# Hybrid attention and mLSTM layer on one core: the first projection block split by k, its neighbour in other PSUM banks

## The chip, the cores and the metric

The kernel runs on one core of one Trainium2 chip. The metric is the device time of one execution in microseconds (us), the median over several executions.

## The reference, cut to what matters

One layer over 256 tokens of width 1024, batch 1. After a norm, a single projection `w_in` gives all inputs of two mixers; its products and four elementwise steps are what the change touches:

```python
h = rms_norm(x, mix_norm_g[layer])
proj = h @ w_in[layer]                     # 1024 -> 5640 features
(q_a, k_a, v_a, q_m, k_m, v_m, o_m, i_m, f_m, g_a, g_m) = jnp.split(proj, split_points, axis=-1)
y_a = from_heads(moba_attention(...))      # 8 heads of 64
qk_m = jax.nn.silu(causal_depthwise_conv(jnp.concatenate([q_m, k_m], axis=-1), conv_qk[layer]))
log_i = (i_m.astype(f32) + b_igate[layer].astype(f32)).transpose(0, 2, 1)
log_f = jax.nn.log_sigmoid(f_m.astype(f32) + b_fgate[layer].astype(f32)).transpose(0, 2, 1)
h_m = mlstm_chunkwise(...)                 # 4 heads of 128
merged = sigmoid(g_a) * (y_a @ w_out_attn) + sigmoid(g_m) * (y_m @ w_out_mlstm)
x = x + merged @ w_o[layer]
h = rms_norm(x, ffn_norm_g[layer])
x = x + (silu(h @ w_ffn_gate[layer]) * (h @ w_ffn_up[layer])) @ w_ffn_down[layer]
return rms_norm(x, final_norm_g)
```

The convolution runs over time, 4 taps wide, on the 512 features of `q_m` and the 512 of `k_m`.

## The kernel before, in words

All products are made in three passes of a rounded type: each operand is split into a high part (`w_hi`, `hT_hi`) and the rest (`w_lo`, `hT_lo`), and hi x hi, hi x lo and lo x hi are summed in PSUM. The 1024 x N weights come in **chunks** of 128 x 2048 numbers (1 MB), 63 in the whole kernel. A chunk c goes through four steps: SyncE loads it into one of three raw buffers (`load`; it waits until the chunk three before has its low part, `lo_ready`), ScalarE copies it to `w_hi` (`split_hi`, `hi_ready`), VectorE subtracts to get `w_lo` (`split_lo`, `lo_ready`), TensorE uses it and counts `chunk_used`. Six slots hold hi and lo parts.

Every engine runs its own list of instructions in the order in which it is written, and waits on counters. ScalarE and VectorE have a loop over chunks c in which the split of chunk c + 4 stands beside the other work of step c.

The order of the blocks is `q_m` (chunks 0 and 1), `k_m` (2, 3), `q_a` (4, 5), `k_a` (6, 7), then token-major blocks. For the first eight chunks the weights are the stationary operand, so a result tile is 128 features x 256 tokens. Chunk 0 holds 256 features and all eight k-tiles. TensorE turns x (8 k-tiles x 2 token tiles, each 128 x 128) into the banks named `xT`; ScalarE scales and rounds them into `hT_hi` (`xT_hi`), VectorE makes `hT_lo` (`xT_lo`). Chunk 0 is loaded in three pieces (two of 256 KB, one of 512 KB); the low parts of the two small ones are made by GpSimd (L385), that of the third by VectorE (L868). While TensorE is in chunk 0, it also transposes `vec_rows`, the convolution's weights (L1259), and VectorE copies them to `vcol` (L872) before `split_lo(1)`. The eight gate columns (`wif`) are split by ScalarE and VectorE (L549, L551, L877) and multiplied in `gates`, after chunk 1.

The convolution of chunk c (0 to 3) is `tap3(c)` on ScalarE and `conv(c)` on VectorE, six instructions (L739, counted by `conv_step`), which read the chunk's PSUM bank. Chunk c + 4 is written to the same bank, and so TensorE waits there: `pe.wait_ge(conv_step, 6 * (c - 3))` for c from 4 to 7. The gate rows (L891 to L895), a logarithm on ScalarE (L562, L564) and the scans over time (L900 to L908) all stand in VectorE's step c == 2. `gate_columns` on TensorE comes after chunk 5 and uses them.

Of the kernel before, what the change touches and what calls it, by code (L numbers as in the profile page):

```python
# [62 lines left out]
def build(nc, x, mix_norm_g, w_in, conv_qk, b_igate, b_fgate, mlstm_norm_g, w_out_attn,  # L63
# [11 lines left out]
    with ExitStack() as ctx:  # L75
# [211 lines left out]
        def _(sp):  # L287
            def load(c, src):
# [138 lines left out]
        def _(act):  # L427
# [23 lines left out]
            def tap3(c):  # L451

                b, h = divmod(c, 2)
                act.wait_ge(chunk_used, c + 1)
                if c == 0:
# [1015 lines left out]
```

## Time and profile before

| | us |
|---|---|
| runs of the kernel before (3) | 394.48 median, 394.45 to 396.41 |
| profiled execution, its own time | 395.16 |
| span of that execution, first to last instruction | 393.1 |
| TensorE busy with products | 381.3 (97%) |
| VectorE busy | 241.7 (62%) |
| ScalarE busy | 199.6 (51%) |
| GpSimd busy | 35.2 (9%) |
| TensorE's first product of chunk 0 starts | 11.03 |

The page gives for each engine how long it was busy. The trace below it lists instructions with their start (us from the start of the span), how long they took, and in brackets how long the engine had been idle and what ended that. The tables of waits and the chain of work that ended last say which wait was the last to end.

### The profile page before, as it was taken

What the parts mean: (1) busy time and instruction counts of PE and PEld (TensorE: products, weight loads), DVE (VectorE), ACT (ScalarE), POOL (GpSimd) and SP (SyncE); (2) the same over time, 40 slices, a digit from 0 to 9 for tenths busy, and PEclk for the clock granted to TensorE, in tenths of its full rate; (3) what the DMA queues carried; (4) which work ended last, traced back from release to release, by engine and by line L of the source; (5) the groups of instructions that cost most, each with busy time, mean ns of one, the idle gap of its engine ahead of it and who ended that gap; (6) DMA issues with size and microseconds to landing.
All of it is one profiled execution on the core that took longest, in us unless ns stands there. A gap on an engine that the chain in (4) does not pass through costs nothing.

```text
span 393.1 us, 5336 instructions
## 1 busy us (share of the span) xinstructions
PE 381.3 (97%) x2101; PEld 326.8 (83%) x2101; DVE 241.7 (62%) x312; ACT 199.6 (51%) x246; POOL 35.2 (9%) x46
## 2 busy tenths in 40 slices
PE   6999999999999999999999999999999999999993
PEld 5999998777888888887878888888888888888882
DVE  2869777748529677569458573735648366472224
ACT  5862997554676546063347472552716437163014
POOL 3896001000000010000110000000000000000002
PEclk9999999999999999999999999999999999999997
DMA  7889076943534589627234848448184572930002
GB/s 248 244 278 306 10 229 226 334 168 113 179 137 152 176 316 321 214 82 243 105 107 159 269 147 281 150 172 267 68 305 128 192 238 85 316 106 1 0 0 108
DMA packets 48697, 70.55 MB, mean 179 GB/s; under 512 B 2300, under 2 KB 33064, under 8 KB 48680
## 3 DMA queue, kind: packets, MB, share of 16 engines
q1 hardware_dynamic: 48520, 70.05, 53.6%
q8 instruction: 12, 0.20, 0.2%
q10 hardware_dynamic: 160, 0.27, 0.2%
q14 instruction: 5, 0.04, 0.0%
HBM read 69.26 MB, written 1.05 MB: 179 GB/s over the span
## 4 chain that ended last, share of the span: by engine, by line
PE 85%; DVE 7%; DMA 3%; ACT 2%; issue 1%; POOL 0%; SPq 0%; POOLq 0%; ACTq 0%
PE pa L1102 19%; PE pp L1111 13%; PE pp L1112 13%; PE pp L1113 13%; PE pa L1104 10%; DVE w_lo L718 3%; PE pa L1111 2%; PE pa L1112 2%; PE pa L1113 2%; DMA w_raw<-in_w_in 2%; DVE region_a L739 2%; DMA x_sb<-in_x 1%; PE pp L1082 1%; ACT w_hi L433 1%; PE pp L1084 1%; PE pp L1083 1%
## 5 line engine op out<-in xcount | busy, mean ns | idle before, releaser
L718 DVE TENSOR_TENSOR w_lo<-w_raw,w_hi 128x2048 fp32r<-128x2048 f32 x38 | 86.8, 2295 | 36.2 <-ACT w_hi L433 36.2
L433 ACT ACTIVATE w_hi<-w_raw 128x2048 fp32r<-128x2048 f32 x38 | 72.8, 1918 | 25.4 <-PE pp L1113 14.8
L1102 PE MATMUL pa<-hT,w_hi 128*128 128x512 f32 x320 | 79.9, 392 | 0.0
L1102 PEld LDWEIGHTS pa<-hT,w_hi 128*128 128x128 f32 x320 | 58.2, 189 | 10.8
L1038 DVE TENSOR_TENSOR w_lo<-w_raw,w_hi 128x2048 fp32r<-128x2048 f32 x24 | 53.6, 2288 | 8.9 <-ACT w_hi L684 8.9
L1111 PE MATMUL pp<-w_hi,hT 128*128 128x512 f32 x128 | 51.1, 400 | 0.0
L1113 PE MATMUL pp<-w_lo,hT 128*128 128x512 f32 x128 | 49.9, 390 | 0.0
L1112 PE MATMUL pp<-w_hi,hT 128*128 128x512 f32 x128 | 49.9, 390 | 0.0
L1104 PEld LDWEIGHTS pa<-hT,w_lo 128*128 128x128 f32 x320 | 43.7, 190 | 3.1
L1104 PE MATMUL pa<-hT,w_lo 128*128 128x256 f32 x320 | 44.6, 282 | 0.0
L684 ACT ACTIVATE w_hi<-w_raw 128x2048 fp32r<-128x2048 f32 x24 | 44.1, 1902 | 0.0
L1111 PE MATMUL pp<-w_hi,yT_hi 128*128 128x512 f32 x104 | 40.7, 391 | 0.0
L1112 PE MATMUL pp<-w_hi,yT_lo 128*128 128x512 f32 x104 | 40.6, 390 | 0.0
L1113 PE MATMUL pp<-w_lo,yT_hi 128*128 128x512 f32 x104 | 40.5, 389 | 0.0
L1021 DVE TENSOR_TENSOR region_a<-pa,region_a 128x512 f32<-128x512 f32 x10 | 6.9, 692 | 44.6 <-ACT region_a L666 44.6
L666 ACT ACTIVATE region_a<-pa 128x512 f32<-128x512 f32 x10 | 6.0, 599 | 47.3 <-PE pa L1104 47.3
L1111 PEld LDWEIGHTS pp<-w_hi,hT 128*128 128x128 f32 x128 | 24.1, 188 | 5.9 <-issue 1.3
L1113 PEld LDWEIGHTS pp<-w_lo,hT 128*128 128x128 f32 x128 | 24.0, 188 | 5.2
L1082 PE MATMUL pp<-hT,w_hi 128*128 128x256 f32 x96 | 27.3, 284 | 0.7 <-DVE region_a L739 0.7
L1112 PEld LDWEIGHTS pp<-w_hi,hT 128*128 128x128 f32 x128 | 24.1, 188 | 4.6
L1084 PE MATMUL pp<-hT,w_lo 128*128 128x256 f32 x96 | 27.2, 283 | 0.0
L1083 PE MATMUL pp<-hT,w_hi 128*128 128x256 f32 x96 | 27.2, 283 | 0.0
(218 smaller groups left out, 524.9 us busy)
## 6 DMA issues: line engine op xcount, KB each, us to landing
w_raw<-in_w_in SPq DMA_DIRECT2D x21, 1024.0 KB, 5.1
w_raw<-in_w_ffn_gate SPq DMA_DIRECT2D x11, 1024.0 KB, 5.4
w_raw<-in_w_ffn_up SPq DMA_DIRECT2D x11, 1024.0 KB, 6.2
w_raw<-in_w_ffn_down SPq DMA_DIRECT2D x11, 1024.0 KB, 6.5
w_raw<-in_w_o SPq DMA_DIRECT2D x4, 1024.0 KB, 5.8
w_raw<-in_w_out_attn SPq DMA_DIRECT2D x2, 1024.0 KB, 5.0
w_raw<-in_w_out_mlstm SPq DMA_DIRECT2D x2, 1024.0 KB, 5.1
x_sb<-in_x SPq DMA_DIRECT2D x4, 256.0 KB, 3.8
```

Source lines behind the costliest of these rows:

```text
L433: nc.scalar.activation(w_hi[:, slot_of(c), :], w_raw[:, c % RAW, :], ACT.Copy).then_inc(hi_ready, 1)
L684: nc.scalar.activation(w_hi[:, slot_of(c + r), :], w_raw[:, (c + r) % RAW, :], ACT.Copy).then_inc(hi_ready, 1)
L718: nc.vector.tensor_tensor(w_lo[:, slot_of(c), :], w_raw[:, c % RAW, :], w_hi[:, slot_of(c), :].bitcast(F32), ALU.subtract).then_inc(lo_rea ...
L1038: nc.vector.tensor_tensor(w_lo[:, slot_of(c + r), :], w_raw[:, (c + r) % RAW, :], w_hi[:, slot_of(c + r), :].bitcast(F32), ALU.subtract).t ...
L1082: mm(o, hi[:, w], hT_hi[:, k, :], start=(k == 0), stop=False)
L1083: mm(o, hi[:, w], hT_lo[:, k, :], start=False, stop=False)
L1084: ins = mm(o, lo[:, w], hT_hi[:, k, :], start=False, stop=(k == KT - 1))
L1102: mm(banks[:, f, :], w_hi[:, s, w[k]], hT[:, k], start=(k == 0), stop=False)
L1104: ins = mm(banks[:, f, 0:S], w_lo[:, s, w[k]], hT_hi[:, k, :], start=False, stop=(k == KT - 1))
L1111: mm(o, aT_hi[:, k, tok], w_hi[:, s, w], start=start, stop=False)
L1112: mm(o, aT_lo[:, k, tok], w_hi[:, s, w], start=False, stop=False)
L1113: return mm(o, aT_hi[:, k, tok], w_lo[:, s, w], start=False, stop=stop)
```

## The change

- **Block 0 split by k.** Chunk 0 now holds k-tiles 0 to 3 for all 512 features of `q_m`, chunk 1 holds k-tiles 4 to 7. All four result tiles grow together, one in the first half of each of the four banks `pp`, over both chunks (`all_tiles`). For each k-tile there are eight products with `w_hi` before the four with `w_lo`.
- **Order on TensorE.** It turns x for k-tiles 0 to 3 of both token tiles and 4 to 7 of the first, then works on chunk 0; the last four transposes (`turn_x(1, 1)`) stand between chunk 0's hi and lo products. The transposes of `vec_rows` move from chunk 0 to chunk 1, behind its hi products.
- **Block 1 (`k_m`)** goes to the banks `pa` 0 and 1, and the waits of chunks 4 to 7 on `conv_step` become 6, 6, 12, 12 (they were 6, 12, 18, 24).
- **Gate rows in two parts.** The first part (the sums up to `row_l`) stands in VectorE's step c == 1, the scans stay in step c == 2. The gates use `pa` 2, `rcol` is turned in `pp` 3.
- **Loads.** x comes in two loads of 512 KB (was four of 256 KB), chunk 0 in two of 512 KB; the vector loads are issued by ScalarE instead of SyncE. Norms change places: ScalarE does the second half of the features, VectorE the first.
- **GpSimd** makes no low parts; VectorE makes both halves of chunk 0's.

```diff
-        xT = [pa[:, 0, 0:S], pp[:, 1, 0:S], pp[:, 2, 0:S], pp[:, 3, 0:S],
-              pa[:, 2, 0:S], pa[:, 3, 0:S], pa[:, 2, S:2 * S], pa[:, 3, S:2 * S]]
-
-        def conv_in(c, f):
-            if c == 0 and f == 1:
-                return pa[:, 1, 0:S]
-            return pp[:, c, f * S:(f + 1) * S]
+        xT = [pa[:, k % 4, k // 4 * S:(k // 4 + 1) * S] for k in range(KT)]
+
+        def conv_in(ft):
+            if ft < 4:
+                return pp[:, ft, 0:S]
+            return pa[:, ft // 2 - 2, ft % 2 * S:(ft % 2 + 1) * S]
...
-                if b < FEATURE_MAJOR:
+                if 0 < b < FEATURE_MAJOR:
                     return w_in_k[:, :, BLOCKS[b] + 256 * h:BLOCKS[b] + 256 * (h + 1)]
                 return w_in_k[:, 4 * h:4 * h + 4, BLOCKS[b]:BLOCKS[b] + 512]
...
-                    sp.wait_ge(piece_lo, 2)
+                    sp.wait_ge(first_half_lo, 1)
                 if c == 0:
-                    for n, loaded in enumerate((*piece_loaded, chunk_loaded[0])):
-                        part = slice(PIECES[n], PIECES[n + 1])
-                        sp.dma_start(as_source(w_raw[:, 0, part], src), src[:, PIECES[n] // 256:PIECES[n + 1] // 256]
-                                     ).then_inc(loaded, 16)
+                    sp.dma_start(as_source(w_raw[:, 0, 0:CH // 2], src), src[:, 0:2]).then_inc(first_half_loaded, 16)
+                    sp.dma_start(as_source(w_raw[:, 0, CH // 2:CH], src), src[:, 2:4]).then_inc(chunk_loaded[0], 16)
...
-            for t in range(T):
-                for h in range(2):
-                    sp.dma_start(x_t[:, t, HALVES[h]], x_d[:, t, HALVES[h]]).then_inc(x_loaded[t][h], 16)
+            sp.dma_start(x_t[:, 0], x_d[:, 0]).then_inc(x_loaded[0], 16)
+            sp.dma_start(x_t[:, 1], x_d[:, 1]).then_inc(x_loaded[1], 16)
             for c in range(C_FFN + 2):
                 load(c, chunk_source(c))
-                if c == 0:
-                    sp.dma_start(vec_rows[0:4, :], mlstm_norm_g.rearrange("a (h p) -> (a h) p", p=P)).then_inc(vec_loaded, 16)
-                    sp.dma_start(vec_rows[4:36, :], conv_qk.rearrange("a j (f p) -> (a j f) p", p=P)).then_inc(vec_loaded, 16)
+                if c == 1:
...
-            for n in range(2):
-                part = slice(PIECES[n], PIECES[n + 1])
-                pool.wait_ge(piece_hi[n], 1)
-                nc.gpsimd.tensor_tensor(w_lo[:, 0, part], w_raw[:, 0, part], w_hi[:, 0, part].bitcast(F32),
-                                        ALU.subtract).then_inc(piece_lo, 1)
...
             nc.scalar.activation(sinv[:, 0:8], minus_half[:, :], ACT.Square)
+            act.dma_start(vec_rows[0:4, :], mlstm_norm_g.rearrange("a (h p) -> (a h) p", p=P)).then_inc(vec_loaded, 16)
+            act.dma_start(vec_rows[4:36, :], conv_qk.rearrange("a j (f p) -> (a j f) p", p=P)).then_inc(vec_loaded, 16)
...
-            norm_half0(0)
-            act.wait_ge(piece_loaded[0], 16)
-            nc.scalar.activation(w_hi[:, 0, 0:512], w_raw[:, 0, 0:512], ACT.Copy).then_inc(piece_hi[0], 1)
-            norm_half0(1)
+            norm_half1(0)
+            act.wait_ge(first_half_loaded, 16)
+            nc.scalar.activation(w_hi[:, 0, 0:512], w_raw[:, 0, 0:512], ACT.Copy).then_inc(row_hi[0], 1)
             act.wait_ge(gcol_set, 1)
             for k in range(4):
                 xT_hi(k)
             act.wait_ge(chunk_loaded[0], 16)
             nc.scalar.activation(w_hi[:, 0, CH // 2:CH], w_raw[:, 0, CH // 2:CH], ACT.Copy).then_inc(hi_ready, 1)
+            norm_half1(1)
+            split_hi(1)
             for k in range(4, KT):
                 xT_hi(k)
-            for c in range(1, AHEAD):
+            for c in range(2, AHEAD):
...
-                if c == 2:
-
-                    act.wait_ge(gate_rows_set, 1)
-                    nc.scalar.activation(row_l, row_l, ACT.Exp).then_inc(exp1_done, 1)
...
+                if c == 3:
+                    tap3(3)
                 split_hi(c + AHEAD)
 
-                if c < 4:
-                    tap3(c)
-                elif c < 8:
+                if c == 1:
+                    tap3(0)
+                    tap3(1)
+
+                    act.wait_ge(gate_rows_set, 1)
+                    nc.scalar.activation(row_l, row_l, ACT.Exp).then_inc(exp1_done, 1)
...
+                elif c == 2:
+                    tap3(2)
...
+            def all_tiles(c, w_part, x_part, k):
+
+                for f in range(4):
+                    o = 512 * (k % 4) + f * P
+                    ins = mm(pp[:, f, 0:S], w_part[:, c, o:o + P], x_part[:, k, :],
+                             start=(k == 0 and w_part is w_hi and x_part is hT_hi),
+                             stop=(k == KT - 1 and w_part is w_lo))
+                return ins
...
+            turn_x(0, 0)
+            turn_x(0, 1)
+            turn_x(1, 0)
...
+                pe.wait_ge(conv_step, 12)
...
+                if c < 2:
+                    for k in range(4 * c, 4 * c + 4):
+                        if k < 2:
+                            pe.wait_ge(row_hi[k], 1)
+                        elif k in (2, 4):
+                            pe.wait_ge(hi_ready, c + 1)
+                        pe.wait_ge(hT_hi_set, k + 1)
+                        all_tiles(c, w_hi, hT_hi, k)
+                        pe.wait_ge(hT_lo_set, k + 1)
+                        all_tiles(c, w_hi, hT_lo, k)
+                    if c == 0:
+                        turn_x(1, 1)
+                    else:
+                        pe.wait_ge(vec_loaded, 32)
+                        nc.tensor.transpose(pa[:, 3, 0:36], vec_rows, ident[0:36, 0:36]).then_inc(vec_turned, 1)
+                    for k in range(4 * c, 4 * c + 4):
+                        if k == 0:
+                            pe.wait_ge(first_half_lo, 1)
+                        elif k in (2, 4):
+                            pe.wait_ge(lo_ready, c + 1)
+                        ins = all_tiles(c, w_lo, hT_hi, k)
                     ins.then_inc(chunk_used, 1)
                 elif b < FEATURE_MAJOR:
                     if b >= 2:
-                        pe.wait_ge(conv_step, 6 * (c - 3))
-                    feature_chunk(c, pp[:, 2 * (b % 2) + h, :]).then_inc(chunk_used, 1)
+                        pe.wait_ge(conv_step, 6 * (b - 1))
+                    if c == 7:
+                        pe.wait_ge(rcol_set, 1)
+                    feature_chunk(c, pa[:, h, :] if b == 1 else pp[:, 2 * (b % 2) + h, :]).then_inc(chunk_used, 1)
```

On VectorE, the start of the program. `w_lo` of 128x1024 is half of chunk 0, of 128x2048 a whole chunk (the first is chunk 1), `hT` rows are the k-tiles of x, `vcol` the convolution's weights, `w_ml` and `yT_hi` the gate columns. Before:

```order
L859 TENSOR_SCALAR region_b<-x_sb,rstd 128x512 [waits rstd_done] x2
L862 CAST w_hi<-w_raw 128x512 [waits piece_loaded1]
L844 SCALAR_TENSOR_TENSOR hT<-pa,gcol,hT 128x256 [waits hT_hi_set,gcol_set]
L844 SCALAR_TENSOR_TENSOR hT<-pp,gcol,hT 128x256 [waits hT_hi_set] x3
L844 SCALAR_TENSOR_TENSOR hT<-pa,gcol,hT 128x256 [waits hT_hi_set] x4
L868 TENSOR_TENSOR w_lo<-w_raw,w_hi 128x1024 [waits hi_ready]
L872 COPY vcol<-pp 128x36 [waits vec_turned]
L718 TENSOR_TENSOR w_lo<-w_raw,w_hi 128x2048 [waits hi_ready]
```

And in the changed kernel:

```order
L845 TENSOR_SCALAR region_b<-x_sb,rstd 128x512 [waits rstd_done] x2
L848 CAST w_hi<-w_raw 128x512 [waits first_half_loaded]
L830 SCALAR_TENSOR_TENSOR hT<-pa,gcol,hT 128x256 [waits hT_hi_set,gcol_set]
L830 SCALAR_TENSOR_TENSOR hT<-pa,gcol,hT 128x256 [waits hT_hi_set] x3
L854 TENSOR_TENSOR w_lo<-w_raw,w_hi 128x1024 [waits row_hi1,row_hi0]
L857 TENSOR_TENSOR w_lo<-w_raw,w_hi 128x1024 [waits hi_ready]
L830 SCALAR_TENSOR_TENSOR hT<-pa,gcol,hT 128x256 [waits hT_hi_set] x4
L863 COPY vcol<-pa 128x36 [waits vec_turned]
L705 TENSOR_TENSOR w_lo<-w_raw,w_hi 128x2048 [waits hi_ready]
```

The low parts of chunk 0 moved ahead of the last four k-tiles; the copy of `vcol` stands, as before, ahead of the low part of chunk 1.

On TensorE, around the transposes of `vec_rows` (`pT`). Before, they stand in chunk 0, ahead of its last eight lo products, and the 32 hi and 16 lo products of chunk 1 follow:

```order
L1259 MATMUL pp<-ident,pT 128x36 [waits vec_loaded]
L1088 MATMUL pp<-hT,w_lo 128x256 [waits lo_ready]
...
L1088 MATMUL pp<-hT,w_hi 128x256 [waits hi_ready,vcol_set]
L1088 MATMUL pp<-hT,w_hi 128x256 x15
L1088 MATMUL pp<-hT,w_lo 128x256 [waits lo_ready]
L1088 MATMUL pp<-hT,w_lo 128x256 x7
L1088 MATMUL pp<-hT,w_hi 128x256 x16
```

And in the changed kernel, from the last k-tile of chunk 1 on:

```order
L1088 MATMUL pp<-hT,w_hi 128x256 [waits hT_lo_set]
L1088 MATMUL pp<-hT,w_hi 128x256 x3
L1263 MATMUL pa<-ident,pT 128x36 [waits vec_loaded]
L1088 MATMUL pp<-hT,w_lo 128x256 [waits lo_ready]
L1088 MATMUL pp<-hT,w_lo 128x256 x15
L1147 MATMUL pa<-hT,yT_hi 100x256 [waits wif_lo_set,wif_hi_set]
```

The transposes moved behind all 32 hi products of chunk 1; only its 16 lo products are left between them and the gates.

## Rows read from the trace of the kernel before

**Rows 1.** Page: span, busy time, VectorE's row of low parts (busy us, mean ns)

```profile
span 393.1 us, 5336 instructions
PE 381.3 (97%) x2101; PEld 326.8 (83%) x2101; DVE 241.7 (62%) x312; ACT 199.6 (51%) x246; POOL 35.2 (9%) x46
...
L718 DVE TENSOR_TENSOR w_lo<-w_raw,w_hi 128x2048 fp32r<-128x2048 f32 x38 | 86.8, 2295 | 36.2 <-ACT w_hi L433 36.2
```

**Rows 2.** Table of waits, TensorE's products (us in total, times, longest)

```profile
PE pa L1136 <- ACT region_b L513: 1.6, 2, 0.8
PE pp L1082 <- DVE region_a L739: 0.7, 1, 0.7
PE pa L1111 <- DVE hT L725: 0.7, 1, 0.7
PE pa L1136 <- DVE region_b L859: 0.3, 1, 0.3
```

**Rows 3.** Timeline, third convolution and chunk 6 (start, us, engine, line; [idle before])

```profile
47.40 2.43 DVE L739 SCALAR_TENSOR_TENSOR region_a<-pp,vcol,region_a 128x255 f32<-128x255 f32 x6
48.99 0.26 PE L1161 MATMUL pa<-ident,v_ml 4*128 4x4 f32 x2
49.98 0.35 PE L1082 MATMUL pp<-hT,w_hi 128*128 128x256 f32 x1 [0.72 <-DVE region_a L739]
```

**Rows 4.** Timeline, TensorE and VectorE, 15 to 26 us

```profile
15.09 1.22 DVE L868 TENSOR_TENSOR w_lo<-w_raw,w_hi 128x1024 fp32r<-128x1024 f32 x1
16.15 0.25 PE L1259 MATMUL pp<-ident,pT 36*128 36x36 f32 x1
16.44 0.20 DVE L872 COPY vcol<-pp 128x36 f32<-128x36 f32 x1
16.55 2.28 DVE L718 TENSOR_TENSOR w_lo<-w_raw,w_hi 128x2048 fp32r<-128x2048 f32 x1
19.15 0.17 DVE L884 COPY w_ml<-w_ml 128x32 f32<-128x32 f32 x1
19.23 2.28 DVE L718 TENSOR_TENSOR w_lo<-w_raw,w_hi 128x2048 fp32r<-128x2048 f32 x1
21.43 0.75 DVE L877 TENSOR_TENSOR yT_hi<-w_ml,yT_hi 128x288 fp32r<-128x288 f32 x1
23.18 0.28 PE L1145 MATMUL pa<-hT,yT_hi 128*100 128x256 f32 x1
25.06 0.28 PE L1082 MATMUL pp<-hT,w_hi 128*128 128x256 f32 x1
```

**Rows 5.** Timeline, all engines, 7 to 12 us

```profile
7.26 0.69 DVE L854 CUSTOM_DVE_ANT_0 o_sb<-x_sb 128x512 f32<-128x512 f32 x1 [1.60 <-DMA x_sb<-in_x]
7.88 0.48 DVE L859 TENSOR_SCALAR region_b<-x_sb,rstd 128x512 f32<-128x512 f32 x1
8.42 0.66 PE L1136 MATMUL pa<-ident,region_b 128*128 128x128 f32 x4 [0.25 <-DVE region_b L859]
9.01 1.27 POOL L385 TENSOR_TENSOR w_lo<-w_raw,w_hi 128x512 fp32r<-128x512 f32 x1
9.08 1.48 DVE L859 TENSOR_SCALAR region_b<-x_sb,rstd 128x512 f32<-128x512 f32 x1 [0.72 <-POOL rstd L379]
9.86 0.33 PE L1136 MATMUL pa<-ident,region_b 128*128 128x128 f32 x1 [0.78 <-ACT region_b L513]
10.29 0.47 ACT L523 ACTIVATE hT<-pa,gcol 128x256 fp32r<-128x256 f32 x1 [0.48 <-PE pa L1136]
10.66 1.20 ACT L523 ACTIVATE hT<-pp,gcol 128x256 fp32r<-128x256 f32 x3
11.03 0.36 PE L1088 MATMUL pp<-hT,w_hi 128*128 128x256 f32 x1
11.73 1.07 ACT L542 ACTIVATE w_hi<-w_raw 128x1024 fp32r<-128x1024 f32 x1
```

**Rows 6.** Stretches of the load phase (first figure us, last two: DMA share, GB/s)

```profile
2.00:7.00 5.00, 4.73 (x24) 4.13 (x22) 0.87 (x3) 2.71 (x7) 0.74 (x2) 1.00 0.91 277
7.00:10.00 3.00, 1.43 (x9) 0.98 (x10) 2.02 (x4) 1.75 (x3) 1.81 (x3) 1.00 1.08 364
```

**Rows 7.** Timeline, small loads' issues, ScalarE ahead of x, GpSimd's long row

```profile
2.73 0.21 ACT L527 ACTIVATE sinv<-minus_half 128x8 f32<-128x8 f32 x1
4.16 0.45 SPq L308 DMA_DIRECT2D pT<-in_mlstm_norm_g  x1
4.65 0.66 SPq L309 DMA_DIRECT2D pT<-in_conv_qk  x1
15.24 15.90 POOL L404 TENSOR_SCALAR alibi<-w_ml 128x384 bf16<-128x384 f32 x8
```

**Rows 8.** Load of a chunk: issue in the timeline, time from issue to landing

```profile
27.46 0.37 SPq L300 DMA_DIRECT2D w_raw<-in_w_in  x1
DMA to landing us min/median/max: 5.3/5.3/5.3
```

**Rows 9.** Timeline, VectorE's gate rows with one row of ScalarE behind

```profile
36.91 0.46 DVE L891 TENSOR_SCALAR o_sb<-pa,b_if 4x256 f32<-4x256 f32 x1
38.79 0.41 DVE L895 SCALAR_TENSOR_TENSOR o_sb<-o_sb 4x256 f32<-4x256 f32 x1
39.23 0.42 ACT L562 ACTIVATE o_sb<-o_sb 4x256 f32<-4x256 f32 x1 [7.37 <-DVE o_sb L895]
```

More of the change, by code:

```diff
@@ L54 @@
 WARM = 23
-PIECES = (0, 512, 1024, CH)
 AHEAD = 4
@@ L194, in build @@
         squares_warm = sem("squares_warm")
-        piece_loaded = [sem(f"piece_loaded{n}") for n in range(2)]
-        piece_hi = [sem(f"piece_hi{n}") for n in range(2)]
-        piece_lo = sem("piece_lo")
+        first_half_loaded = sem("first_half_loaded")
+        row_hi = [sem(f"row_hi{k}") for k in range(2)]
+        first_half_lo = sem("first_half_lo")
         vec_turned = sem("vec_turned")
@@ L449, in turn_hi, with tap3 @@
                                          banks[b].rearrange("p (k n) -> p k n", k=4), ACT.Copy).then_inc(hT_hi_set, 1)
[L451 to L455, printed above, removed]
+            def tap3(n):
+                act.wait_ge(chunk_used, max(n + 1, 2))
+                if n == 0:
                     act.wait_ge(vcol_set, 1)
-                for f in range(2):
-                    ft = 4 * b + 2 * h + f
+                for ft in (2 * n, 2 * n + 1):
                     col = 4 + 3 * 8 + ft
-                    ins = nc.scalar.activation(qk_m[:, ft, :], conv_in(c, f),
-                                               ACT.Copy, scale=vcol[:, col:col + 1])
+                    ins = nc.scalar.activation(qk_m[:, ft, :], conv_in(ft), ACT.Copy, scale=vcol[:, col:col + 1])
                 ins.then_inc(tap3_done, 1)
@@ L858, in _ @@
                 dve.wait_ge(rstd_done, t + 1)
-                nc.vector.tensor_scalar(rb_t[:, t, HALVES[1]], x_t[:, t, HALVES[1]], rstd[:, t:t + 1], None,
-                                        ALU.mult).then_inc(half1_normed, 1)
-            dve.wait_ge(piece_loaded[1], 16)
-            nc.vector.tensor_copy(w_hi[:, 0, 512:1024], w_raw[:, 0, 512:1024]).then_inc(piece_hi[1], 1)
+                nc.vector.tensor_scalar(rb_t[:, t, HALVES[0]], x_t[:, t, HALVES[0]], rstd[:, t:t + 1], None,
+                                        ALU.mult).then_inc(half0_normed, 1)
+            dve.wait_ge(first_half_loaded, 16)
+            nc.vector.tensor_copy(w_hi[:, 0, 512:1024], w_raw[:, 0, 512:1024]).then_inc(row_hi[1], 1)
             dve.wait_ge(gcol_set, 1)
-            for k in range(KT):
+            for k in range(4):
                 xT_lo(k)
+            dve.wait_ge(row_hi[0], 1)
+            dve.wait_ge(row_hi[1], 1)
+            nc.vector.tensor_tensor(w_lo[:, 0, 0:CH // 2], w_raw[:, 0, 0:CH // 2],
+                                    w_hi[:, 0, 0:CH // 2].bitcast(F32), ALU.subtract).then_inc(first_half_lo, 1)
             dve.wait_ge(hi_ready, 1)
@@ L869, in _ @@
                                     w_hi[:, 0, CH // 2:CH].bitcast(F32), ALU.subtract).then_inc(lo_ready, 1)
+            for k in range(4, KT):
+                xT_lo(k)
             dve.wait_ge(vec_turned, 1)
-            nc.vector.tensor_copy(vcol[:, :], pp[:, 1, 0:36]).then_inc(vcol_set, 1)
+            nc.vector.tensor_copy(vcol[:, :], pa[:, 3, 0:36]).then_inc(vcol_set, 1)
             for c in range(1, AHEAD):
@@ L1128, in _, with turn_x @@
                     pe.wait_ge(gain_loaded, 16)
-                    nc.tensor.transpose(pp[:, 1, 0:KT], gain_rows, ident[0:KT, 0:KT]).then_inc(gain_turned, 1)
+                    nc.tensor.transpose(pa[:, 3, 0:KT], gain_rows, ident[0:KT, 0:KT]).then_inc(gain_turned, 1)
                 nc.tensor.transpose(pp[:, 0, 0:P], ident[:, :], ident[:, :])
             pe.wait_ge(gcol_set, 1)
-            for t in range(T):
-                for k in range(KT):
-                    if k in (0, 4):
-                        pe.wait_ge((half0_normed, half1_normed)[k // 4], t + 1)
+            def turn_x(t, h):
+                pe.wait_ge((half0_normed, half1_normed)[h], t + 1)
+                for k in range(4 * h, 4 * h + 4):
                     ins = nc.tensor.transpose(xT[k][:, t * P:(t + 1) * P], rb_t[:, t, k * P:(k + 1) * P], ident[:, :])
```

103 lines of the change are left out of this document (33 added, 70 removed).

## The prediction

> **What bounds the kernel now.** I read the page first, then the waits of TensorE, then the timeline of the first 63 us. TensorE is busy for 381.3 of 393.1 us [rows 1]; the reader is to see that no other engine is near that, so the time moves only where TensorE starts earlier or waits less. The table of its waits shows where: while x is turned it waits 1.6 + 0.3 us, and later there are only two single waits of 0.7 us, one for a convolution (L1082), one for a norm (L1111) [rows 2]. The L1082 wait, counted from start to start, is 49.98 - 48.99 less the 0.2 to the usual next start: 0.8 us [rows 3]. All else is product after product: the convolution's transposes at 16.15, the gates at 23.18, chunk 2 at 25.06 [rows 4]. Between the gates and chunk 2 lie 16 products: 1.88 / 16 = 0.12 us each, also what one of chunk 0 or 1 costs.
>
> So I follow one number, the start of chunk 2 (25.06 before), and then ask which later waits change.
>
> **Part 1: the start, a gain.** Before, x is complete at about 7.24 (VectorE's square starts at 7.26), the norm of the second token tile starts at 9.08, and takes 1.48 us where the same instruction took 0.48 at 7.88 [rows 5]. It ends 0.3 us after GpSimd's subtraction (9.01 + 1.27), which began just ahead of it. The change takes that subtraction away, 1.0 us. It also lets products begin when k-tiles 0 to 3 of the second tile are turned. From x complete: 1.84 to the norm's start, 0.48 norm, 0.06 to the first transpose (8.42, of 7.88 + 0.48), 0.43 until ScalarE reads it (9.86 to 10.29), 0.47 for the high part, 0.05: 3.33 us [rows 5]. Before, it was 11.03 - 7.24 = 3.79, with the first high part ready at 10.76 and TensorE still turning.
>
> When is x complete? Two loads instead of four, issued 0.9 us sooner. From 2 to 7 us the loads moved 277 GB/s [rows 6], and 1.05 MB at that rate from 2.1 on would end at 5.9. Before it was 7.24, since over 0.3 MB of weights had been moved beside it (277 KB/us x 5 us less 1.05 MB). I take 6.5, between both, and keep 5.8 and 7.24 as ends. First product: 6.5 + 3.33 = 9.85.
>
> The Trainium skill (SBUF — State Buffer, "Who interferes with whom") says that VectorE's tensor_scalar and copy can use the ports that GpSimd needs too, and that whichever starts first holds them for its whole instruction; by that rule, the trace agrees with 1.48 against 0.48 us. It also speaks against the full gain, since GpSimd's memsets of `row_one` and `sel` now start with the norm.
>
> No row shows a memset beside such a norm. Bounds: 0, and the 1.0 us that the subtraction cost. VectorE's subtractions at 16.55 and 19.23 ran in 2.28 us each beside GpSimd's row of eight from 15.24 on [rows 4, 7], no longer than the mean of 38 (2.295) [rows 1]; I take 0.1 by these, and keep 1.0 for the range. First product 9.95.
>
> **Part 2: chunks 0 and 1 up to the transposes.** Ahead of the transposes of `vec_rows` now stand 32 + 16 + 32 = 80 products (before, 40): 9.6 us, and four transposes of x, 0.45. One new wait: k-tile 2 needs the high part of the chunk's second half, which ScalarE makes after four `xT_hi`. The first of these starts 0.5 before the first product, the four take 1.6 (0.4 each, 1.20 for 3), the copy 1.07 [rows 5]: ready 2.2 us after the first product, wanted after 1.92, so 0.3 us. The low parts of chunk 0 (two of 1.22 us on VectorE [rows 4]) are ready 4.2 us after the first product and wanted at 4.6; `xT_hi(4)`, behind `split_hi(1)`, is ready 5.4 after it and wanted at 6.5: both hidden, the second as long as chunk 1 lands by 14. The move of the two vector loads to ScalarE's queue costs nothing: its issues, 0.45 and 0.66 us on SyncE before, start after ScalarE's instruction at 2.73 and end near 4.1 [rows 7], and x's first half, 0.52 MB at 277 GB/s from 2.1 on, is there at 4.0 at the earliest. Transposes of `vec_rows` at 9.95 + 9.6 + 0.45 + 0.3 = 20.3 (before 16.15). Call this V.
>
> **Part 3: what hangs on V, the loss.** VectorE copies `vcol` ahead of `split_lo(1)`, and the copy waits for these transposes. Before, they came 7.0 us ahead of the gates, and 56 products covered VectorE's work. Now only the 16 lo products of chunk 1 stand behind them, and these need `split_lo(1)` itself. VectorE's row of instructions after V, by before's starts [rows 4]: `vcol` at +0.3, `split_lo(1)` from +0.4 to +2.7, two copies of gate columns, `split_lo(2)` from +3.08, the gates' low part from +5.28 to +6.03. So TensorE waits from V + 0.2 to V + 2.7 (2.5 us), works until V + 4.65, and waits for the gates' low part until V + 6.1 (1.45 us). Then the gates, 1.9: chunk 2 starts at V + 8.0 = 28.3, against 25.06. That is +3.2 us. While TensorE waits, VectorE has been idle for 3 us ahead of V, having nothing it may do: that is the mechanism, and it costs 3.95 us, more than the start gives.
>
> **Part 4: up to chunk 8.** The wait of 0.8 us for the third convolution goes, if the new chain holds. The load of chunk 4 waits for `split_lo(1)`: issued at V + 2.75, landed 5.3 later [rows 8], V + 8.0. Chunk 5 follows 3.1 behind, V + 11.1. VectorE: `split_lo(4)` to V + 12.2; first part of the gate rows, 2.3 (36.91 to 39.23) [rows 9], to V + 14.5; `split_lo(5)`, 2.25, to V + 16.8; the first convolution, 2.43 [rows 3], done at V + 19.2. Chunk 4 needs it at V + 8.0 + 96 x 0.12 = V + 19.5. It fits with 0.3 us to spare. The second convolution ends at V + 21.6, the scans (2.8) and their answer from ScalarE at V + 25.3, `split_lo(6)` at V + 27.6; chunk 6 wants convolutions 0 and 1 and `split_lo(6)` at V + 32.1. What is late next is `split_lo(7)`, V + 34.7, wanted at V + 39. Nothing waits. The four waits in the middle are worth 0.8 us and no more, for TensorE had no other.
>
> After that TensorE is just later than before by the sum, the other engines less so, and the 0.7 us at L1111 hangs on TensorE's own work and stays.
>
> **Sum.** +3.2 - 0.8 = +2.4 us. Against the profiled execution, 395.16, 397.6; against the median of the runs, 394.48, 396.9.
>
> **Rivals.**
> 1. *x lands early* (the one that isn't slower). If x is complete at 5.8, V is 19.6, and the sum +1.7: 396.2, within 0.5%. For it speaks the rate in [rows 6]; against it, that x was behind that rate before. It decides from 6.05 on down (sum below 1.97, which is 0.5%). For a gain, V would have to be under 17.9, with x complete at 4.1, when its bytes can't be there. The same 396.2 or less comes if the wait at L1111 goes too.
> 2. *GpSimd holds the norm up.* If memsets and selects cost the norm up to 1.0 us, and x is no earlier than before (7.24), V is 22, the sum +4.1: 398.6.
> 3. *The middle chain is late.* If `split_lo(5)` or the loads of chunks 4 and 5 come more than 0.3 us late, chunk 4 waits for the first convolution; if they come 1.3 late, it costs 1.0: 397.9.
> 4. *The clock.* All windows before, at the start too, show a granted clock of 1.00 [rows 6], 2.4 GHz, with waits of at most 1.1 us. A wait of 2.5 us has no row here. At 1.2 GHz the 32 products behind the two waits would cost twice 0.12 each: +3.8, 400.7. The Trainium skill (TensorE: Matmul & The Clock Gate, "HAM oscillation — how this bites in real kernels") says that idle gaps can send the clock to half rate; no run here shows it.
> 5. *The change doesn't do what it says*: the first product no earlier than 11, because the chunk's first half or its copy is late. V 21.4, +3.5: 398.0.
>
> **Chances.** Forecast (x at 6.2 to 7, 396.6 to 397.4) 0.5; rival 1 0.25; rivals 2 and 5 0.12; rival 3 0.07; rival 4 0.03; a gain that I don't see 0.03. A measurement of this kernel can tell about 0.5% from no change, which ends at 396.45. Faster 0.03; within 0.5% 0.31 (rival 1, and the lower edge of the forecast); slower 0.66. The range is 395.9 (rival 1 with 0.3 us more) to 398.3 (most of rivals 2, 3 and 5).
>
> **What would show it.** First product of chunk 0 at 9.9, with the second norm at 0.48 us (part 1). Transposes of `vec_rows` near 20.3, VectorE idle before them for about 3 us, TensorE waiting for the low part of chunk 1 for 2.5 us, then for that of the gates for 1.4 (parts 2 and 3). Chunk 2 at 28.3. No wait of chunks 4 to 7 for a convolution (part 4). I am wrong if TensorE goes through chunk 1 without a wait, or if the first product comes before 8.

## The result: 5.4 us slower, with two waits of 2.5 us and a stretch at half clock

The changed kernel takes 400.11 us (median of 4 runs, 399.99 to 400.18), the kernel before 394.74 beside it (394.45 to 396.41): ratio 1.0131, interval 1.0114 to 1.0148. The profiled execution took 399.99, with a span of 397.9. The direction is as forecast, the size is not: +5.4 where +2.4 was forecast, and 400.11 lies above the range.

From the page of the changed kernel, beside [rows 1]: TensorE's busy time rose by 2.1 us, though it has as many instructions, and the 38 low parts of the weights cost VectorE 0.4 us more in all.

```profile
span 397.9 us, 5330 instructions
PE 383.4 (96%) x2101; PEld 329.0 (83%) x2101; DVE 243.7 (61%) x313; ACT 198.9 (50%) x246; POOL 26.6 (7%) x44
...
L705 DVE TENSOR_TENSOR w_lo<-w_raw,w_hi 128x2048 fp32r<-128x2048 f32 x38 | 87.2, 2307 | 33.0 <-ACT w_hi L420 33.0
```

Its table of TensorE's waits, beside [rows 2] (us in total, times, longest). The convolution's wait is gone; two new ones of 2.5 us stand on top. L1127 is a transpose of the identity at the very start, before x is there; the kernel before has the same wait.

```profile
PE pp L1088 <- DVE w_lo L705: 2.5, 1, 2.5
PE pa L1147 <- DVE yT_hi L868: 2.5, 1, 2.5
PE pp L1127 <- POOL ident L363: 1.6, 1, 1.6
PE pa L1108 <- DVE hT L712: 0.7, 1, 0.7
PE pp L1088 <- ACT hT L503: 0.4, 1, 0.4
```

The chain of work that ended last, its start (start, us, what). From the transposes on it runs through VectorE, as part 3 said; the copy into `w_ml` takes 1.00 where the forecast had about 0.4 us for two such copies, and the low part behind it is 0.8 us longer than the same work was:

```profile
9.58 4.12 PE pp L1088 x32
14.14 5.75 PE pp L1088 x48
20.22 2.28 DVE w_lo L705
22.50 1.00 DVE w_ml L874
23.58 3.09 DVE w_lo L705
```

VectorE in the timeline of the changed kernel, beside [rows 4, 5] (start, us; in brackets the idle time before and what ended it):

```profile
5.45 0.69 DVE L840 CUSTOM_DVE_ANT_0 o_sb<-x_sb 128x512 f32<-128x512 f32 x1 [0.22 <-DMA x_sb<-in_x]
7.52 0.96 DVE L845 TENSOR_SCALAR region_b<-x_sb,rstd 128x512 f32<-128x512 f32 x1 [0.45 <-POOL rstd L371]
8.40 0.86 DVE L848 CAST w_hi<-w_raw 128x512 fp32r<-128x512 f32 x1
...
20.11 0.20 DVE L863 COPY vcol<-pa 128x36 f32<-128x36 f32 x1 [4.01 <-PE pa L1263]
20.22 2.28 DVE L705 TENSOR_TENSOR w_lo<-w_raw,w_hi 128x2048 fp32r<-128x2048 f32 x1
22.42 1.08 DVE L874 COPY w_ml<-w_ml 128x32 f32<-128x32 f32 x1
23.41 0.17 DVE L875 COPY w_ml<-w_ml 128x32 f32<-128x32 f32 x1
23.50 3.17 DVE L705 TENSOR_TENSOR w_lo<-w_raw,w_hi 128x2048 fp32r<-128x2048 f32 x1
26.60 0.44 DVE L868 TENSOR_TENSOR yT_hi<-w_ml,yT_hi 128x288 fp32r<-128x288 f32 x1
```

The four idle microseconds ahead of `vcol` are followed on TensorE by waits for `w_lo` (from about 20.0 to 22.55) and `yT_hi` (to 27.19). The low part that took 3.17 us took 2.28 before, and the copy that took 1.08 took 0.48 before and takes 0.47 in e1 below. GpSimd's timeline shows what ran beside them: its row of eight starts 4.8 us sooner (10.45, 15.24 before), since GpSimd makes no low parts now, and it is done in 10.23 us where it took 15.90 [rows 7]. So the two selects behind it, which started at 31.30 before, fall between 20.83 and 24.53, onto VectorE's one critical stretch.

```profile
10.45 10.23 POOL L391 TENSOR_SCALAR alibi<-w_ml 128x384 bf16<-128x384 f32 x8
20.83 3.70 POOL L395 TENSOR_SCALAR_AFFINE_SELECT alibi<-alibi 128x1024 bf16<-128x1024 bf16 x2
```

And TensorE, the gates and the start of chunk 2 (start, us; a product takes a place of 0.12 us between starts, here it becomes 0.21):

```profile
27.19 0.33 PE L1147 MATMUL pa<-hT,yT_hi 128*100 128x256 f32 x1 [2.46 <-DVE yT_hi L868]
27.36 0.28 PE L1148 MATMUL pa<-hT,yT_hi 128*100 128x256 f32 x1
...
28.43 0.41 PE L1147 MATMUL pa<-hT,yT_hi 128*100 128x256 f32 x1
28.65 0.41 PE L1148 MATMUL pa<-hT,yT_hi 128*100 128x256 f32 x1
...
29.71 0.41 PE L1079 MATMUL pa<-hT,w_hi 128*128 128x256 f32 x1
29.93 0.41 PE L1080 MATMUL pa<-hT,w_hi 128*128 128x256 f32 x1
```

The table of stretches for the same place (us; then busy time and number of instructions of PE, PEld, DVE, ACT, POOL; the granted clock; DMA share and GB/s). The clock is the figure behind POOL's: 1.00, then 0.69, 0.50, 0.60, and 1.00 again. 0.50 is 1.2 GHz.

```profile
27.00:28.00 1.00, 0.81 (x7) 0.84 (x8) 1.00 (x2) 0.00 (x0) 0.00 (x0) 1.00 0.75 194
28.00:29.00 1.00, 1.00 (x8) 1.00 (x7) 1.00 (x1) 0.76 (x1) 0.00 (x0) 0.69 0.77 187
29.00:30.00 1.00, 1.00 (x7) 1.00 (x6) 0.24 (x1) 1.00 (x1) 0.00 (x0) 0.50 1.07 382
...
31.00:32.00 1.00, 1.00 (x7) 1.00 (x7) 1.00 (x1) 0.00 (x0) 0.00 (x0) 0.60 1.10 348
32.00:33.00 1.00, 1.00 (x10) 1.00 (x10) 0.99 (x3) 0.91 (x1) 0.00 (x0) 1.00 1.10 351
```

The marks along TensorE, read from both timelines (starts, us):

| | before | after | difference |
|---|---|---|---|
| first product of chunk 0 | 11.03 | 9.58 | -1.45 |
| transposes of `vec_rows` (V) | 16.15 | 19.82 | +3.67 |
| gates | 23.18 | 27.19 | +4.01 |
| chunk 2 | 25.06 | 29.71 | +4.65 |
| chunk 3 | 30.81 | 36.38 | +5.57 |
| chunk 6 | 49.98 | 54.76 | +4.78 |
| chunk 8 | 62.87 | 67.67 | +4.80 |
| last product | 385.95 | 390.78 | +4.83 |

All of the loss is made by chunk 3 and 0.8 of it is given back at chunk 6. The spans differ by 4.8, the medians by 5.4; the profiled execution of before lies 0.4 above its median, that of after 0.1 below.

### The profile page after: what moved, and what is told of

It is laid out like the page before. It is cut to its first block, busy times and chain, and to the rows that moved or that the text cites. A ratio compares the mean times of both kernels' runs of the same rounds, so it can differ in the third digit from the quotient of the medians.

```text
span 397.9 us, 5330 instructions
## 1 busy us (share of the span) xinstructions
PE 383.4 (96%) x2101; PEld 329.0 (83%) x2101; DVE 243.7 (61%) x313; ACT 198.9 (50%) x246; POOL 26.6 (7%) x44
## 4 chain that ended last, share of the span: by engine, by line
PE 94%; DVE 3%; ACT 1%; issue 0%; POOL 0%; POOLq 0%; ACTq 0%
PE pa L1099 18%; PE pp L1108 13%; PE pp L1109 13%; PE pp L1110 13%; PE pa L1101 10%; PE pp L1088 2%; PE pp L1079 2%; PE pp L1080 2%; PE pp L1081 2%; DVE w_lo L705 2%; PE pa L1108 2%; PE pa L1110 2%; PE pa L1109 2%; PE pp L1127 1%; PE pa L1079 1%; PE pa L1080 1%
## 5 line engine op out<-in xcount | busy, mean ns | idle before, releaser
L1110 PEld LDWEIGHTS pp<-w_lo,yT_hi 128*128 128x128 f32 x104 | 19.5, 188 | 4.1
L1108 PEld LDWEIGHTS pp<-w_hi,yT_hi 128*128 128x128 f32 x104 | 19.6, 188 | 3.8
L1109 PEld LDWEIGHTS pp<-w_hi,yT_lo 128*128 128x128 f32 x104 | 19.6, 188 | 3.6
```

The costliest lines, as they stand in the source:

```text
L1108: mm(o, aT_hi[:, k, tok], w_hi[:, s, w], start=start, stop=False)
L1109: mm(o, aT_lo[:, k, tok], w_hi[:, s, w], start=False, stop=False)
L1110: return mm(o, aT_hi[:, k, tok], w_lo[:, s, w], start=False, stop=stop)
```

## The experiments

The theory after the result had three parts: the copy of `vcol` ahead of `split_lo(1)` makes both waits; GpSimd's selects lengthen the second; the waits bring the clock down. The rivals were that transposing later is bad in itself, that the clock falls for another reason, and that the division of block 0 has a cost of its own. Each edit is to the changed kernel unless it says otherwise.

### The copy of vcol behind the low parts (e1)

```diff
-            dve.wait_ge(vec_turned, 1)
-            nc.vector.tensor_copy(vcol[:, :], pa[:, 3, 0:36]).then_inc(vcol_set, 1)
             for c in range(1, AHEAD):
                 split_lo(c)
...
+            dve.wait_ge(vec_turned, 1)
+            nc.vector.tensor_copy(vcol[:, :], pa[:, 3, 0:36]).then_inc(vcol_set, 1)
```

> The changed kernel, with one thing moved: on VectorE the copy of vcol (with its wait for the transposes of vec_rows) stands behind the low parts of chunks 1 to 3 instead of ahead of that of chunk 1. Theory A (the order on VectorE is the whole loss: two waits of 2.5 us on TensorE, and 16 products at half the clock after them): the low part of chunk 1 runs from 16.1 to 18.4, that of chunk 2 to 21.4, TensorE has no wait in chunk 1 and none at the gates, the clock stays at 1.00, chunk 2 starts at 23.9 instead of 29.9: 400.1 - 6.0 = 394.1 us. Theory B (the chain of loads, low parts and convolutions behind it takes the gain back): TensorE then waits 1 us or more for a convolution at chunks 4 to 7, and the time is 395.5 or more.

Measured: 393.52 us (11 runs, 393.27 to 394.07), 394.95 for before beside it, ratio to before 0.9961, 0.9947 to 0.9975. Both waits are gone, and the clock stays at 1.00. This kernel's waits of TensorE:

```profile
PE pp L1127 <- POOL ident L363: 1.6, 1, 1.6
PE pa L1134 <- DVE region_b L845: 0.7, 2, 0.5
PE pa L1108 <- DVE hT L712: 0.7, 1, 0.7
PE pp L1088 <- ACT hT L503: 0.4, 1, 0.4
```

VectorE does the low parts of chunks 1 and 2 in the time in which it stood idle in the changed kernel, beside GpSimd's row, which is nearly back at its old length; the selects then start at 25.94, behind the gates' low part (timeline of this kernel):

```profile
16.07 2.27 DVE L705 TENSOR_TENSOR w_lo<-w_raw,w_hi 128x2048 fp32r<-128x2048 f32 x1
18.75 2.28 DVE L705 TENSOR_TENSOR w_lo<-w_raw,w_hi 128x2048 fp32r<-128x2048 f32 x1
24.69 0.18 DVE L875 COPY vcol<-pa 128x36 f32<-128x36 f32 x1
...
10.57 15.22 POOL L391 TENSOR_SCALAR alibi<-w_ml 128x384 bf16<-128x384 f32 x8
```

V, the start of the transposes of `vec_rows`, is at 19.95, as late as in the changed kernel (19.82), yet the gates start at 22.15, chunk 6 at 48.16 (49.98 before), chunk 8 at 61.08. So late transposes cost nothing in themselves; one line's place costs 6.6 us. The change with this line moved is faster than both kernels.

### The transposes sooner (e2)

```diff
                         all_tiles(c, w_hi, hT_lo, k)
+                        if k == 4:
+                            pe.wait_ge(hT_lo_set, KT)
+                            pe.wait_ge(vec_loaded, 32)
+                            nc.tensor.transpose(pa[:, 3, 0:36], ...).then_inc(vec_turned, 1)
```

(and away from behind chunk 1's hi products.) To put them back into chunk 0 wasn't tried, since their bank still holds turned x there.

> The changed kernel, with the transposes of vec_rows put behind k-tile 4 of chunk 1 on TensorE instead of behind its hi products, so 2.9 us sooner; VectorE's order as in the changed kernel. Theory A: vcol at 17.2, the low part of chunk 1 ready at 19.6, ahead of its use at 20.1, so the first wait of 2.5 us goes; the gates' low part is ready near 23.7 and TensorE is there at 22.0, so 1.8 us of the second wait stay and the clock stays at 1.00. Chunk 2 at 25.7: 400.1 - 4.2 = 395.9 us. Theory B: a convolution is late at chunk 4, 397 or more.

Measured: 394.65 (394.49 to 394.86), ratio 0.9985, 0.9972 to 0.9999. V is at 17.16, the wait for `w_lo` is gone, and the one for the gates' low part is 1.0 us:

```profile
PE pa L1147 <- DVE yT_hi L868: 1.0, 1, 1.0
```

Undoing part of the move takes back 5.5 us and brings the time to that of before, by the same mechanism as e1: it is the distance from V to the work that waits for VectorE. After this gap of 1.0 us the clock stayed at 1.00. The time is 1.2 us under what I expected: with a wait of 1.0 and not 1.8, chunk 2 starts at 25.35 and not at 25.7, and my sum ended there, so it left out the 0.9 us that the clock costs the changed kernel within chunk 2.

### Work in the gaps, no wait removed (e3)

```diff
+                        for _ in range(18):
+                            nc.tensor.transpose(pa[:, 1, 0:P], ident[:, :], ident[:, :])
...
                 if c == 1:
+                    for _ in range(18):
+                        nc.tensor.transpose(pa[:, 1, 0:P], ident[:, :], ident[:, :])
                     gates()
```

> The changed kernel, with 18 idle transposes of the identity (into a bank that nobody reads) on TensorE behind the transposes of vec_rows, and 18 more ahead of the gates, 0.11 us each, so about 2 us of work within each wait of 2.5 us. The waits end when they did, since VectorE's rows are unchanged. Theory A (the half clock from 28.3 to 31.7 comes of TensorE standing still twice): the clock stays at 1.00, 16 products cost 0.12 instead of 0.21 us, 400.1 - 1.6 = 398.5 us. Rival (the half clock has another cause, or idle transposes don't help): 400.1 us.

Measured: 398.78 (398.47 to 399.25), ratio 1.0086, 1.0064 to 1.0108. VectorE's work is what it was (the gates start at V + 7.37 in both), so what differs behind it is the clock. This kernel's stretches:

```profile
24.00:28.00 4.00, 3.51 (x31) 3.31 (x31) 4.00 (x3) 2.46 (x3) 0.85 (x1) 1.00 0.83 260
28.00:32.00 4.00, 4.00 (x36) 4.00 (x35) 3.53 (x2) 2.74 (x3) 0.00 (x0) 1.00 1.03 313
```

The clock is 1.00 throughout. The median is 1.3 under the changed kernel's, with a first product 0.3 later; chunk 2 comes 1.93 behind the gates (2.52 in the changed kernel), chunk 3 5.77 behind that (6.67). TensorE's two waits are down to 0.4 and 0.5 us. The idle gaps bring the clock down, and that is worth 0.6 + 0.9 us. So 36 more instructions on the busiest engine made this kernel faster.

### GpSimd's selects later (e4)

```diff
             link(ins)
+            pool.wait_ge(wif_lo_set, 1)
             for lo in (0, 256):
```

> The changed kernel, with GpSimd's two selects on alibi (1.85 us each, 20.8 to 24.5) waiting for the gates' low part. Theory A (the low part of chunk 2 took 3.17 instead of 2.28 us since a select held it up): it takes 2.28 again, the copy ahead of it 0.5 instead of 1.08, TensorE's wait for the gates is 1.0 to 1.4 us instead of 2.5: 398.7 to 399.1 us with the half clock as it was, 397.3 if the shorter wait keeps the clock up too. Rival (the 3.17 us have another cause, loads for example): 400.1 us.

Measured: 397.63 (397.44 to 398.26), ratio 1.0060, 1.0037 to 1.0082. VectorE's instructions are back at their lengths:

```profile
22.44 0.17 DVE L875 COPY w_ml<-w_ml 128x32 f32<-128x32 f32 x1
22.61 2.29 DVE L706 TENSOR_TENSOR w_lo<-w_raw,w_hi 128x2048 fp32r<-128x2048 f32 x1
```

The selects' part is shown: the copy and the low part are shorter by 0.91 and 0.88 us, 1.8 in all, and the gates start at 25.98 instead of 27.19. The clock fell all the same, and sooner, after the first wait alone (2.5 us for `w_lo`). This kernel's stretches:

```profile
22.00:23.00 1.00, 0.42 (x3) 0.42 (x4) 1.00 (x4) 0.27 (x1) 0.00 (x0) 0.91 0.00 0
23.00:24.00 1.00, 1.00 (x6) 1.00 (x6) 1.00 (x1) 1.00 (x3) 0.00 (x0) 0.50 0.37 45
...
26.00:27.00 1.00, 1.00 (x9) 1.00 (x9) 1.00 (x1) 0.00 (x0) 1.00 (x1) 0.89 1.09 385
```

Here the slow stretch falls on chunk 1's 16 lo products, where it costs little: they take 3.4 us, from 22.58 to 25.98, instead of about 1.9, but at full clock TensorE would have waited for the gates' low part until about 25.4 (it is written from 24.81 to 25.26). So the clock costs 0.6 there and 0.1 in the gates, 0.7 instead of the changed kernel's 1.6; chunk 2 takes 5.75 us. That is why this kernel gained 2.5 us where the selects alone are worth 1.8. The time is close to the 397.3 that I expected for a clock that stays up, but the clock did not stay up.

### The old waits of chunks 4 to 7 (e5), and the gate rows in one part (e9)

Both include e1's edit. e5 puts back the wait of before:

```diff
-                        pe.wait_ge(conv_step, 6 * (b - 1))
+                        pe.wait_ge(conv_step, 6 * (c - 3))
```

> The kernel of the run with the vcol copy behind, and in it the old waits of chunks 4 to 7 for the convolution: 6, 12, 18, 24 steps instead of 6, 6, 12, 12. In that kernel's trace the third convolution ends at 45.4 and the fourth at 47.8, and TensorE starts chunk 6 at 47.8 and chunk 7 at 54.9. Theory: the four looser waits are worth nothing by themselves; the wait of 0.8 us at chunk 6 went because VectorE gets to the third convolution 4.4 us sooner (gate rows in two parts, low part of chunk 1 not held up): 393.5 us, no difference. Rival, the one of the prediction (the looser waits are what is worth 0.8 us): 394.3 us.

Measured: 393.67 (393.26 to 394.06), ratio 0.9967, 0.9954 to 0.9979; e1 has 393.52. No wait appears. The looser waits, to which the prediction gave the 0.8 us, are worth nothing measurable here. In the changed kernel itself the old waits were not tried; its last two convolutions run from 47.48 to 52.24, and chunk 6 starts at 54.76, so they would not have held it up there.

e9 is e5 with the first part of the gate rows, and ScalarE's exponential and logarithm behind it, back in step c == 2 (VectorE's part of the edit):

```diff
-                if c == 1:
+                if c == 2:
                     dve.wait_ge(gates_done, 1)
```

> The run with the vcol copy behind and the old waits for the convolution (6, 12, 18, 24), and in it the gate rows undivided again: their first part and the logarithm in step 2 instead of 1. Of the change, the block split by k and the banks are then what is left in the middle part. Theory (the third convolution comes sooner by 2.1 us since VectorE no longer waits for ScalarE's table load and logarithm, and by 2.3 us since the loads of chunks 3 and 4 are issued sooner): VectorE stands idle for 2.2 us before the scans again, the third convolution ends at 47.5 instead of 45.4, still ahead of chunk 6 at 48.1, so TensorE doesn't wait: 393.6 us, no difference. Rival (the divided gate rows are what took the 0.8 us away): TensorE waits at chunk 6 for the convolution, 394.3 us.

Measured: 395.6 (393.68 to 397.61), ratio 1.0016, 0.9992 to 1.0041: so wide that the time decides nothing. The trace, of the execution of 393.68, does show a step. VectorE stands idle for ScalarE in the middle of the gate rows, the third convolution runs from 45.89 on, and chunk 6 waits for it:

```profile
39.90 0.41 DVE L893 SCALAR_TENSOR_TENSOR o_sb<-o_sb 4x256 f32<-4x256 f32 x1 [2.21 <-ACT o_sb L547]
45.89 4.77 DVE L726 SCALAR_TENSOR_TENSOR region_a<-pa,vcol,region_a 128x255 f32<-128x255 f32 x12
```

and from this kernel's table of TensorE's waits:

```profile
PE pp L1080 <- DVE region_a L726: 0.4, 1, 0.4
```

In e1, with the rows divided, the same convolution starts at 43.04. So of the 0.8 us that chunk 6 waited before, the division of the gate rows is worth about 0.4 in the trace. I expected no wait here. The other 0.4 has two sides: from before to e9 VectorE's gate rows come 1.5 us sooner (36.91, 35.40), but without the wait TensorE would be at chunk 6 only 1.2 us sooner (49.26, 48.09). Which edit makes this difference is open.

### The start: GpSimd's memsets (e6), four loads of x (e7), the subtraction of before (e8)

e6 is e1 with GpSimd's memsets and selects behind the norm and the cast:

```diff
+            pool.wait_ge(half0_normed, 2)
+            pool.wait_ge(row_hi[1], 1)
             nc.gpsimd.memset(row_one, 1.0).then_inc(ones_set, 1)
```

> The kernel with the vcol copy behind, and GpSimd's memset of row_one, with all that follows on GpSimd, waiting until VectorE has done both norms and its copy of the chunk's second row. Theory (GpSimd's memsets and selects made the second norm 0.96 and the copy 0.86 us long): they take 0.48 and 0.41 again, the first product of chunk 0 starts 0.5 us sooner, and the time is 393.0 to 393.2 us. Rival (these two are long for another cause, the loads for example): 393.5 us.

Measured: 393.42 (393.03 to 394.29), ratio 0.9961, 0.9947 to 0.9975, the same as e1. In the trace the norm and the cast, 0.96 and 0.86 us in the changed kernel, take half as long, and the first product starts at 9.13 instead of e1's 9.71; the span is 0.5 shorter (390.8, 391.3). The effect on the instructions is shown; that it reaches the time is not.

```profile
7.54 0.49 DVE L847 TENSOR_SCALAR region_b<-x_sb,rstd 128x512 f32<-128x512 f32 x1 [0.45 <-POOL rstd L371]
7.94 0.42 DVE L850 CAST w_hi<-w_raw 128x512 fp32r<-128x512 f32 x1
8.48 0.30 POOL L376 MEMSET w_ml<- 4x256 f32 x1 [0.98 <-DVE w_hi L850]
```

e7 is e1 with x in four loads:

```diff
-            sp.dma_start(x_t[:, 0], x_d[:, 0]).then_inc(x_loaded[0], 16)
-            sp.dma_start(x_t[:, 1], x_d[:, 1]).then_inc(x_loaded[1], 16)
+            for t in range(T):
+                for h in range(2):
+                    sp.dma_start(x_t[:, t, HALVES[h]], x_d[:, t, HALVES[h]]).then_inc(x_loaded[2 * t + h], 16)
```

> The kernel with the vcol copy behind, and x in four loads of 256 KB again, issued from 0.8 to 2.3 us, ahead of the weights. Theory (x was complete at 5.4 instead of 7.2 since two large loads leave less room for weights to go ahead of it): x is complete about 1 us later, the first product starts at 10.2 instead of 9.4, 394.2 us. Rival (x was complete sooner for another cause, such as fewer small loads on the same queue): 393.5 us.

Measured: 394.25 (393.95 to 395.7), ratio 0.9989, 0.9976 to 1.0001; e1 has 393.52. VectorE's square of the second token tile starts at 6.62 (5.58 in e1), the first product at 10.50 (9.71 in e1):

```profile
6.62 0.69 DVE L841 CUSTOM_DVE_ANT_0 o_sb<-x_sb 128x512 f32<-128x512 f32 x1 [1.39 <-DMA x_sb<-in_x]
```

Two loads instead of four are worth 0.8 us at the first product, and the medians agree with it (0.7). Why x is there sooner isn't shown: in e7 the last load of x and the weights' loads behind it are also issued later.

e8 is an edit of the kernel before: GpSimd's subtractions wait for the second norm.

```diff
                 part = slice(PIECES[n], PIECES[n + 1])
+                pool.wait_ge(half1_normed, 2)
                 pool.wait_ge(piece_hi[n], 1)
```

> The kernel before, with one wait more: GpSimd's two subtractions for the low parts of chunk 0 wait until both norms are done. Theory (the first subtraction made the second norm 1.48 instead of 0.48 us long): the norm takes 0.48, the first product starts at 10.4 to 10.6 instead of 11.03, and since nothing else is late by that, the time falls by about 0.5 us: 394.4 us against 394.95. Rival (VectorE's chain of low parts and convolutions, which ended the wait at chunk 6, doesn't move with it): the wait at chunk 6 grows by the same 0.5 us, no difference.

Measured: 395.19 (394.4 to 396.31), ratio 1.0004, 0.9989 to 1.0018. The norm of 1.48 us [rows 5] takes 0.49, as part 1 had it, and the first product starts at 10.35 (11.03). Chunk 8 starts 0.66 sooner than before (62.21), the span is 0.3 shorter, and the time can't be told from before's: the 0.5 us that I expected is seen in the marks and not in the median.

```profile
8.53 0.49 DVE L860 TENSOR_SCALAR region_b<-x_sb,rstd 128x512 f32<-128x512 f32 x1 [0.72 <-POOL rstd L379]
```

The wait at chunk 6 is still there, in its table of waits:

```profile
PE pp L1083 <- DVE region_a L740: 0.6, 1, 0.6
```

## Why the prediction was right in direction and wrong in size

Two terms of the sum carry the miss. The second wait of part 3 was put at 1.45 us and measured 2.46. The clock was put at nothing in the sum and cost 1.6 us. The rest came out within 0.5 us.

**Part 1, the start: nearly right as a sum, wrong in its terms.** Forecast 9.95, measured 9.58. x was complete at about 5.43, under the low end of 5.8 (the sum there gives 5.9): the rate of [rows 6], 277 GB/s, was a mean over five microseconds, and was no bound. From 3 to 5 us the changed kernel moved 390 and 367 GB/s. Against it, the chain from there was 4.15 us instead of 3.43, with 0.4 of the difference in the norm (0.96 instead of 0.58) and 0.2 ahead of it, where the norm started 2.1 us after x and not 1.84, for GpSimd was done with the first tile's scale only at 6.56. A cast behind the norm took 0.86, and both ran beside GpSimd's memsets and selects. e6 shows that these held them up: the value I took, 0.1, had been read from subtractions, which are another kind of instruction.

**Part 2: right.** V was forecast at 20.3 and came at 19.82; from the first product it was 10.24 against 10.35. The wait of 0.3 us for k-tile 2 didn't show: the chain has 32 products in a row. The small vector loads were issued at 1.50 and 1.79, not after 2.73 as assumed, and that did no harm.

**Part 3, the waits: the mechanism right, the second wait mis-sized.** The first wait was forecast at 2.5 us and was 2.5; the idle time of VectorE ahead of V was 4.0, forecast about 3. The second was forecast at 1.45 and was 2.46, with the gates at V + 7.37 instead of V + 6.1. The step that failed is "by before's starts": VectorE's durations were carried over from a stretch in which GpSimd was in its long row, and GpSimd's row was taken to stay where it was. But GpSimd, without its low parts, starts its row 4.8 us sooner, and a VectorE that idles for 4 us lets it through the row in 5.7 us less. The selects met the critical stretch by both: in e1, with the first alone, they start at 25.94, behind it, and a row of 10.23 us from 15.24 on would have ended at about 25.5 (an estimate from these figures). e4 shows what they cost: 1.8 us. The miss is only 1.3, since without the selects the stretch is 0.6 shorter than before's (in e4 the gates' low part takes 0.45, not 0.75, and the first copy 0.17, not 0.48).

The Trainium skill (SBUF — State Buffer, "Who interferes with whom") says that a VectorE instruction with two inputs in SBUF contends with a GpSimd instruction that reads SBUF, and that the one which started first keeps the shared ports to its end. The trace agrees: the second low part began at 23.50, a select ended at 24.53, and the low part took 0.89 us more than the 2.28 of its like. The first low part, which began before the selects, was not longer; the first select, beside it, took 2.63 us where the second took 1.11.

**The clock, rival 4, was left out of the sum.** It had a chance of 0.03 and a price of 3.8 us. It happened, at 1.56: six places of the gates (2.52 us instead of 1.88) and ten of chunk 2 (6.67 instead of 5.75) ran at about half rate, then the clock was back. "No row here" was taken as a reason for a small chance, where it was a reason for a wide range; and the price assumed that 16 products behind each of the two waits run slow, where the clock fell once. e3 shows cause and price.

**Part 4: right in what happened, wrong in why.** No chunk waited for a convolution, and the 0.8 came back at chunk 6. VectorE's marks held: the low part of chunk 4 ended at V + 12.7 (forecast 12.2), the first convolution at V + 19.5 (19.2). As chunk 4 was itself late by the selects and the clock (42.15, V + 22.3), the slack that was forecast at 0.3 us was 2.8. But e5 shows that the looser waits weren't needed, and e9 that the divided gate rows gave about half. Put with the rest: 2.4 (forecast) - 0.5 (V) + 1.3 (the stretch with the selects) + 1.6 (clock) = 4.8, beside 4.8 in the span.

**Rivals 1, 2, 3 and 5** each named something real or absent by itself: x did come early (rival 1, its condition met), the norm was held up by 0.5 us (rival 2), the middle chain wasn't late (3), and the first product was in time (5). None of them was the miss.

## What to carry to other kernels

When a producer is moved later, look at what stands behind its consumer in that engine's list: here one small copy held back a megabyte's low part, and moving the copy behind six instructions turned a change of +5.4 us into one of -1.4. When an engine idles where it was busy, re-time the engine that it slows and that slows it (GpSimd here), for that one's next work arrives sooner and meets something else. A new wait on the bounding engine of 2.5 us should be priced with the clock at half rate behind it as well (1.6 us here), and the experiment that tells the two apart is to fill the gap with work that nobody needs.

## What the runs showed of the hardware that I had not expected

- After one idle stretch of 2.5 us on TensorE, out of steady work, the clock fell to 0.50 (e4). In the changed kernel it was down for about 3.3 us (28.3 to 31.6), with places of 0.21 us instead of 0.12. In the changed kernel it fell only after the second of two such waits; why not after the first, no run here tells. A wait of 1.0 us left it at 1.00 (e2). The Trainium skill (TensorE: Matmul & The Clock Gate, "HAM oscillation — how this bites in real kernels") has idle gaps as the cause, and e3 agrees.
- Transposes of the identity into an unused bank kept the clock at 1.00 (e3).
- VectorE and GpSimd slow each other both ways: eight instructions of GpSimd took 10.23 us with VectorE idle for part of them, 12.96 in e2, 15.22 in e1 and 15.90 before. One of the eight takes 1.17 us with VectorE idle, and up to 2.71 beside a low part (e1).
- Memsets and selects of at most 36 rows on GpSimd beside a norm of VectorE doubled its time (0.96 for 0.49) and that of a cast (0.86 for 0.42); e6 has them apart.
- x in two loads of 512 KB was complete 1.0 us sooner than in four of 256 KB (VectorE's second square starts at 5.58 in e1, at 6.62 in e7).
